# Expert rows scattered in item order and read back by plain transfers, in a two-layer decoder step

## What is computed

```
logits = h @ w_router + b_router;  probs = softmax(logits)
group  = the one of 4 expert groups whose two best probs sum highest
gates  = the two best experts of that group, weighted to sum 1
y = sum over the two experts e:  gates[e] * ((silu(h @ w_gate[e]) * (h @ w_up[e])) @ w_down[e])
```

## Time and profile before

| | us |
|---|---|
| median of 3 runs | 2256.04 |
| lowest, highest | 2251.12, 2267.28 |
| profiled execution, its own time | 2252.14 |
| its span (first to last instruction) | 2250.4 |

### The profile page before, as it was taken

How to read it: one execution, slowest core, us unless ns; L and a number is a source line. 1 busy time by engine, 2 the same in 40 slices (tenths; PEclk the granted TensorE clock), 3 DMA queues, 4 the chain that set the end, 5 groups by cost and what they waited for, 6 DMA issues and landing times.

```text
span 2250.4 us, 22594 instructions
## 1 busy us (share of the span) xinstructions
PE 1770.5 (79%) x7649; PEld 1214.5 (54%) x7649; DVE 1216.2 (54%) x1760; ACT 860.5 (38%) x1035; POOL 221.7 (10%) x242
## 2 busy tenths in 40 slices
PE   3799898889898994299999179995577942999990
PEld 0556335565335774187877057663344742787870
DVE  1332344332335337398988572237733373989886
ACT  1222222222223202088887212223343022887861
POOL 0000000000010000322221200000000003122201
PEclk7799999899999995599999589976776956999995
DMA  8344184344173423399998512122001243999973
GB/s 306 142 170 171 56 289 161 128 164 171 56 280 113 142 95 113 103 347 393 393 393 330 197 57 75 60 81 75 1 1 38 68 178 130 368 393 392 393 292 123
DMA packets 199192, 418.66 MB, mean 186 GB/s; under 512 B 16909, under 2 KB 21069, under 8 KB 199094
## 3 DMA queue, kind: packets, MB, share of 16 engines
q1 hardware_dynamic: 169730, 322.26, 40.2%
q0 software_dynamic: 22128, 73.53, 8.8%
q10 hardware_dynamic: 7254, 21.84, 2.9%
HBM read 367.56 MB, written 50.03 MB: 186 GB/s over the span
## 4 chain that ended last, share of the span: by engine, by line
PE 59%; DVE 14%; DMA 10%; issue 5%; ACT 4%; DVEq 4%; POOL 1%; ACTq 1%; POOLq 0%; SPq 0%
PE bank L652 24%; PE bank L998 18%; PE bank L636 3%; DMA RING<-in_w_in_ret 3%; PE bank L936 3%; DMA RING<-in_w_gate 2%; PE bank L674 2%; ACT WH L1478 2%; PE bank L921 1%; PE bank L910 1%; DVEq L2415 1%; DVE RINGR L1866 1%; POOL slot_d L1764 1%; DVE X L1925 1%; DVE X L1923 1%
## 5 line engine op out<-in xcount | busy, mean ns | idle before, releaser
L2260 DVE TENSOR_TENSOR WL<-RING,WH 128x2048 fp32r<-128x2048 f32 x192 | 435.8, 2289 | 71.4 <-ACT WH L1478 69.6
L652 PE MATMUL bank<-RINGR,HTH 128*128 128x512 f32 (+2 forms) x1440 | 468.9, 410 | 2.9 <-ACT M L1403 2.3
L1478 ACT ACTIVATE WH<-RING 128x2048 fp32r<-128x2048 f32 x192 | 364.5, 1915 | 113.4 <-PE bank L998 92.8
L636 PE MATMUL bank<-cst,M 128*128 128x128 f32 (+3 forms) x721 | 124.1, 307 | 263.9 <-DMA M<-h_d,slot_c 81.2
L652 PEld LDWEIGHTS bank<-RINGR,HTH 128*128 128x128 f32 (+1 forms) x1440 | 249.0, 181 | 117.1 <-issue 34.2
L652 PE MATMUL bank<-RINGR,HTL 128*128 128x512 f32 (+3 forms) x720 | 288.7, 402 | 0.0
L636 PEld LDWEIGHTS bank<-cst,M 128*128 128x128 f32 (+3 forms) x721 | 99.0, 164 | 298.0 <-DMA M<-h_d,slot_c 81.4
L1866 DVE TENSOR_TENSOR RINGR<-RING,RINGR 128x2048 fp32r<-128x2048 f32 (+1 forms) x48 | 105.8, 2211 | 225.5 <-ACT RINGR L1279 198.9
L998 PE MATMUL bank<-WH,HGH 128*128 128x512 f32 x512 | 204.4, 399 | 3.0 <-DVE HGL L2271 3.0
L998 PE MATMUL bank<-WH,HGL 128*128 128x512 f32 x512 | 201.3, 393 | 0.0
L998 PE MATMUL bank<-WL,HGH 128*128 128x512 f32 x512 | 200.9, 392 | 0.0
(11 more groups left out here) (285 smaller groups left out, 2417.2 us busy)
## 6 DMA issues: line engine op xcount, KB each, us to landing
RING<-in_w_gate SPq DMA_DIRECT2D x64, 1024.0 KB, 11.0
RING<-in_w_up SPq DMA_DIRECT2D x64, 1024.0 KB, 12.2
RING<-in_w_down SPq DMA_DIRECT2D x64, 1024.0 KB, 11.0
RING<-in_w_mod SPq DMA_DIRECT2D x48, 1024.0 KB, 7.5
RING<-in_w_in_ret SPq DMA_DIRECT2D x24, 1024.0 KB, 9.3
RING<-in_state_ret SPq DMA_DIRECT2D x16, 1024.0 KB, 7.1
out_ret_sample<-RING POOLq DMA_DIRECT2D x16, 1024.0 KB, 6.6
RING<-in_w_in_dsa SPq DMA_DIRECT2D x10, 1024.0 KB, 5.1
```

Source lines behind the costliest of these rows:

```text
L636: last = pe.transpose(d_, s_, ident[0:r, 0:r])
L652: last = pe.matmul(out, x_[:, c, :], w_[:, c, :], start=start and c == n == 0, stop=stop and c == 3 and n == 2)
L1478: act.activation(WH[:, u % SPLIT, :, :], raw(u % RAW), ACT.Copy).then_inc(S("hi_rdy"), 1)
L2260: TT(WL[:, u % SPLIT, :, :], raw(u % RAW), WH[:, u % SPLIT, :, :].bitcast(F32), ALU.subtract)\
```

## The change

The buffer `h_d` becomes as large as `y_d`, 128 x 24 rows of 4 KB, and is filled with zeros at the start, behind the fill of `y_d` and on the same semaphore; the two waits for `y_zero` ask for both. POOL no longer stores the tiles of h, and no token numbers are kept. When the destinations are known (`dest_rdy`, a new semaphore ahead of the rest of `route`), ten indirect transfers scatter the rows of `HN` itself to both destinations. For each item a plain transfer on POOL's queue then reads its 128 rows, 96 KB apart; a small copy of zeros and the drain in front of it stay. `HN` has five buffers, over `WL`'s units 2 and 3 and the first row buffer, so VectorE makes the low parts of units 2 and 3 only after the first `take_rows` and after `scattered`. In layer 1's `modulate` a wait for the stores of k and v is added, since `HN` lies over them; the input `tok` isn't loaded.

```diff
-N_CONST = 5
+N_CONST = 4
...
-        h_d = dram("h_d", (TOK, D))
-        slot_d = dram("slot_d", (P * ITEMS, 1), I32)
+        h_d = dram("h_d", (P * ITEMS, D))
+        h_items = h_d.rearrange("(p i) d -> p i d", i=ITEMS)
...
-        HN = [view(2 * SPLIT * UW, D), view(2 * SPLIT * UW + D, D)]
+        HN = [view((2 * SPLIT - 2) * UW + t * D, D) for t in range(TILES)]
...
                     if mod_at == EARLY:
-                        act.wait_ge(S("y_zero"), 16)
+                        act.wait_ge(S("y_zero"), 32)
                     take_part(mod_at, MP[mod_at % 2], bank[7])
...
-            act.dma_start(tok[:, :], A["tok"]).then_inc(S("const_in"), 16)
...
-            pool.dma_start(slot_d.rearrange("(p i) o -> p (i o)", p=P), zero_i[:, :]).then_inc(S("slot_zero"), 16)
+            pool.dma_start(h_items, zero_f.rearrange("p (o d) -> p o d", o=1).to_broadcast([P, ITEMS, D])).then_inc(S("y_zero"), 16)
...
             def experts(l):
                 m = 2 * l + 1
-                for t in range(TILES):
-                    pool.wait_ge(S("hn"), TILES * m + t + 1)
-                    pool.dma_start(h_d[cols(t), :], HN[t % 2][0:rows(t), :]).then_inc(S(f"h_st{t % 2}"), 16)
-                pool.wait_ge(S("slot_zero"), 16)
-                pool.wait_ge(S("tables"), l + 1)
+                pool.wait_ge(S("y_zero"), 32)
+                pool.wait_ge(S("dest_rdy"), l + 1)
                 for k in range(2):
                     for t in range(TILES):
                         R = rows(t)
-                        pool.indirect_dma_start(out=slot_d, out_offset=bass.IndirectOffsetOnAxis(ap=dest_i[0:R, k, t:t + 1], axis=0),
-                                                in_=tok[0:R, t:t + 1], in_offset=None).then_inc(S("scattered"), 16)
+                        pool.indirect_dma_start(out=h_d, out_offset=bass.IndirectOffsetOnAxis(ap=dest_i[0:R, k, t:t + 1], axis=0),
+                                                in_=HN[t][0:R, :], in_offset=None).then_inc(S("scattered"), 16)
+                pool.wait_ge(S("tables"), l + 1)
                 pool.wait_ge(S("scattered"), 16 * 2 * TILES * (l + 1))
-                pool.dma_start(slot_i[:, :], slot_d.rearrange("(p i) o -> p (i o)", i=ITEMS)).then_inc(S("slots_in"), 16)
-                for par in range(2):
-                    pool.wait_ge(S(f"h_st{par}"), 16 * (l + 1) * tiles_of[par])
-                pool.wait_ge(S("slots_in"), 16 * (l + 1))
                 first, last = pairs(pool, l)
                 def gather(j, k):
                     pool.wait_ge(S(f"hg_ps{j}"), (first + k) * 2 + 2)
-                    nc.gpsimd.tensor_tensor(slot_c[:, j:j + 1], slot_i[:, bass.ds(k * 2 + j, 1)], zero_i[:, 0:1], ALU.add)
+                    nc.gpsimd.tensor_tensor(turn_c[:, j:j + 1], zero_i[:, 0:1], zero_i[:, 0:1], ALU.add)
                     pool.drain()
-                    pool.indirect_dma_start(out=HG[j], out_offset=None, in_=h_d,
-                                            in_offset=bass.IndirectOffsetOnAxis(ap=slot_c[:, j:j + 1], axis=0))\
-                        .then_inc(S(f"rows_in{j}"), 16)
+                    item = k * 2 + j
+                    src = h_items[:, item:item + 1, :] if isinstance(item, int) else h_items[:, bass.ds(item, 1), :]
+                    pool.dma_start(HG[j], src.rearrange("p o d -> p (o d)")).then_inc(S(f"rows_in{j}"), 16)
...
             def modulate(m, t):
                 if t == 0:
                     dve.wait_ge(S("bc_in"), 64 * m + 64)
+                    if m == 3:
+                        dve.wait_ge(S("kv_st"), 16 * 3 * TILES)
...
-                if t >= 2:
-                    dve.wait_ge(S("ht_ps"), 2 * TILES * m + 2 * (t - 1))
-                    if m % 2:
-                        dve.wait_ge(S(f"h_st{t % 2}"), 16 * ((m // 2) * tiles_of[t % 2] + t // 2))
...
-                    dve.tensor_copy(dest_i[:, k, :], r1)
+                    last = dve.tensor_copy(dest_i[:, k, :], r1)
                     D_()
+                last.then_inc(S("dest_rdy"), 1)
...
-                first = pairs_before(dve, l)
-                for u in range(SPLIT):
-                    low_unit(first, u)
+                start = pairs_before(dve, l)
                 first, last = pairs(dve, l)
...
-                take_rows(0, first)
+                for u in range(SPLIT):
+                    if u == 2:
+                        take_rows(0, first)
+                        dve.wait_ge(S("scattered"), 16 * 2 * TILES * (l + 1))
+                    low_unit(start, u)
                 with dve.Fori(0, last) as k:
                     pair(first + k, False)
```

More of the change, by code:

```diff
@@ L187, in trunk @@
         rotc = sb("rotc", [P, 2, TILES, P])
-        tok = sb("tok", [P, TILES], I32)
         zero_i = sb("zero_i", [P, ITEMS], I32)
@@ L200, in trunk @@
         np_i = sb("np_i", [P, DEPTH], I32)
-        slot_i = sb("slot_i", [P, ITEMS], I32)
-        slot_c = sb("slot_c", [P, 2], I32)
+        turn_c = sb("turn_c", [P, 2], I32)
         dest_c = sb("dest_c", [P, 2, TILES], I32)
@@ L714, in modulated @@
                         transposes([bank[6 + g][:, q * R:(q + 1) * R] for q in range(4)],
-                                   [HN[t % 2][0:R, (4 * g + q) * P:(4 * g + q + 1) * P] for q in range(4)], "ht_ps")
+                                   [HN[t][0:R, (4 * g + q) * P:(4 * g + q + 1) * P] for q in range(4)], "ht_ps")
                     if m % 2 and t:
@@ L1850, in modulate @@
                     dve.wait_ge(S("bc_in"), 64 * m + 64)
+                    if m == 3:
+                        dve.wait_ge(S("kv_st"), 16 * 3 * TILES)
                 R = rows(t)
                 sc_, sh = (SC[:, 0, :], SC[:, 1, :]) if t == NT else SCALE_SHIFT if m else (BC[:, 0, :], BC[:, 1, :])
-                if t >= 2:
-                    dve.wait_ge(S("ht_ps"), 2 * TILES * m + 2 * (t - 1))
-                    if m % 2:
-                        dve.wait_ge(S(f"h_st{t % 2}"), 16 * ((m // 2) * tiles_of[t % 2] + t // 2))
-                TT(HN[t % 2][0:R, :], X[0:R, t, :], sc_[0:R, :], ALU.mult)
+                TT(HN[t][0:R, :], X[0:R, t, :], sc_[0:R, :], ALU.mult)
                 dve.drain()
-                TT(HN[t % 2][0:R, :], HN[t % 2][0:R, :], sh[0:R, :], ALU.add).then_inc(S("hn"), 1)
+                TT(HN[t][0:R, :], HN[t][0:R, :], sh[0:R, :], ALU.add).then_inc(S("hn"), 1)
             def low(*key):
```

## The result

The changed kernel takes 2276.85 us in the median of seven executions (2269.28 to 2279.77), the kernel before 2256.04 us (2251.12 to 2267.28). The ratio is 1.0088, with a 95% interval of 1.0070 to 1.0106: slower by 0.9%, some 20 us. The forecast was 2273 us. The profiled execution took 2269.28 us, its span is 2267.7 us, 17.3 more than before; the granted clock is 0.865 in the mean, 0.867 before.

A forecast was written before the change was run, and what follows sets the result against it. No engine was taken to bound the kernel throughout; the experts' loop runs at the transfers' pace. Fill +25, gain before the experts -8, loop 0 make +17 us on the 2256.0 us median: 2273 us, range 2256 to 2287.

The forecast's parts named there:

- The fill (+25): Start of layer 0: ScalarE waits for the 12.58 MB fill until 122 us, delaying its split by 25 us.
- Whether loads or fill go first hardly matters: Start of layer 0: the order of fill and ring loads is nearly indifferent, since ScalarE needs both before its split.
- No place where the delay is caught up: After the start of layer 0: nothing later absorbs the fill's delay, so all +25 us stay.
- Rival (a): Later slack absorbs the fill's delay, leaving only the 8 us gain: 2248 us; sign: split under 8 us late; chance 0.10.
- The gain before the experts (8 us): Routing to first expert rows: 4.0 us shorter in layer 0, 4.7 in layer 1, less about 0.3 each; 8 us.
- I take a gain of 0.8 here in layer 0 and 1.5 in layer 1: Before the experts: the last row scatter lands 0.8 us earlier in layer 0 and 1.5 us earlier in layer 1.
- The read-back (2.2 us): Before the experts: reading back the token table and issuing that read go away, saving 2.2 us a layer.
- The standing time: Before the first rows: POOL's standing between small copy and first row transfer stays 7.20 and 4.40 us; other end 0.83.
- (b): Before the experts: the ten row scatters land 5 us later a layer than taken, +27, 2283 us; chance 0.20.
- (c): Before the experts: POOL's standing time belongs to the table's transfers and falls to 0.83 us, +7, 2263 us; chance 0.14.
- (d): Experts' loop: plain reads of rows 96 KB apart take twice as long, adding 43 us, 2316 us; chance 0.03.
- The loop (0): Experts' loop: same bytes at the pace of the transfers, so no change, within 5 us either side.

The follow-up runs named there:

- experiment 1: The kernel before plus only the 12 MB zero fill, into a buffer nothing reads, and the wait for both fills: 2280.75 us against 2253.88, ratio 1.0105.
- experiment 2: The changed kernel with the large fill from its own zero tile and semaphore, ScalarE waiting for the first fill alone, bias rows behind it: 2280.24 us, one execution.
- experiment 3: The changed kernel with the large fill on its own tile and semaphore, and the two bias rows issued ahead of it: 2265.16 us, one execution.
- experiment 7: The changed kernel with VectorE waiting for `scattered` before all four low halves, not only the last two: span 2261.8 us, one execution.
- experiment 6: The changed kernel without the small copy and drain ahead of each layer's first two row transfers: span 2260.3 us, one execution.
- experiment 9: The changed kernel with one more drain on POOL, ahead of its waits for the routing: 2271.21 us, span 2269.6 us, one execution.
- experiment 10: The kernel before with one more drain on POOL, behind the five stores of h: 2247.93 us against 2255.86, ratio 0.9966.

## Why the prediction was right, and where not

**The fill (+25): right.** Measured +23.9 at the split and, in experiment 1, the whole loss. The fill and the loads moved their 13.4 MB at 418 to 420 GB/s and not at the 393 of the loop's mix, and the wait ended at 120.7 and not at 122. The bias rows in POOL's queue, named in the text, are worth 3 to 5 us of it (experiments 2 and 3, one execution each).

**"Whether loads or fill go first hardly matters": right for the change, wrong as a rule.** It holds because ScalarE needs both. It hid that the loads get a third of the bytes beside the fill and not half, since the two move equal numbers of packets, of 2 and of 4 KB, which is why taking the wait away alone gave back little (experiment 2), and why my own expectation of 104 us there failed.

**No place where the delay is caught up: right.** Rival (a) decided at a split less than 8 us late; it was 23.9 late. 22 of it were still there at 300 us, so some 2 us of slack there was, right behind the split. What shrank later, 3.3 us, was the clock's, not slack in the work.

**The gain before the experts (8 us): the right sign, half the size.** Measured 4.3 us. The term that failed is "I take a gain of 0.8 here in layer 0 and 1.5 in layer 1" for the last scatter. It landed 21.4 us after the last `dest_i` and not 20.6: 0.8 later. The issue was right: it starts 0.9 us after the last `dest_i` and not 3.0, two are slow where I took three, and the last comes 14.4 us after the last `dest_i`, as worked out (14.3), but I had let the transfers run at 393 GB/s throughout. They fell to 262 and 101 beside the slow issues (experiment 7), with no rows at all from 934 to 936 us, and the last scatter took 6.97 us to land. Second, the plain transfer of rows took 4.0 us and not the 3.2 that I took from the 2.9 us of the earlier trace rows; the gathers' own 4.12 and 4.26 were the nearer rows. The read-back (2.2 us) went as counted. The standing time fell by 0.5 in each layer, which the prediction kept whole; the six transfers that POOL no longer issues explain it.

**Rivals.** (b), scatters 5 us later a layer than taken, was true in part: the last lands 1.6 us later than taken in layer 0 and 2.6 in layer 1 (22.1 us after the last `dest_i`, where it was 21.0 before and 1.5 less was taken). (c), the standing time belongs to the table, was false: it is the drain's (experiments 6, 9 and 10), and stayed. (d), the wide pitch: no sign of it, the loop's rate is unchanged and a row transfer takes what a gather took.

**The loop (0): right.** From the first `HGL` to the landing of the last store the two kernels differ by 0.3 us in layer 0 and 0.8 in layer 1.

**The total.** Forecast 2273, measured 2276.85. By the profiled executions +17.3 was measured and +17 forecast, but the measured terms are +23.9 and -4.3, which make 19.6. The fill was taken 1.1 us too high and the gain 3.7 too high, and the 2.3 us between 19.6 and 17.3 are the clock's steps and the little slack behind the split. That the two totals meet within 0.3 us is luck; the medians differ by 20.8.

## What to carry to other kernels

A large fill or copy is not free because its data isn't needed for long: put it where the trace shows the transfers idle, since beside weight loads it takes most of the rate and the load is what comes late. If the two must meet, compare the sizes of their packets: in these traces each queue got as many packets as the other, so the one with the larger packets got the bytes. Look for a standing time between an instruction and the next transfer in which neither an engine nor a queue moves: here it was a drain whose time grew with the transfers issued since the last drain, and one more drain in an idle stretch took 8 us off. Where the issue of indirect transfers lies on the path, keep VectorE's two-input work, and the loads that it releases, out of that stretch.

## What was not expected of the hardware

- Three ring loads of 1 MB beside the fill of 12 MB had 134 of 410 GB/s; a load took some 29 us and not 10. Beside three copies from HBM to HBM of 4 MB one took 43.66 us. In both cases the two queues moved nearly equal numbers of packets (1011 and 1013, 273 and 271), of 2 KB for the loads, 4 KB for the fill and up to 32 KB for the copies.
- POOL's drain takes about 0.63 us and 0.082 us for each transfer that POOL has issued since its last drain, also for those that have long landed: 7.20 us for 80, 1.45 for 10, 1.56 for 11. Four kernels had less, as though a 12 MB fill had cleared up what lay before it (5.05 us with 74, 54 of them behind the fill).
- The drain also waits for a transfer of POOL's in flight: between the first two row transfers of layer 0 stands one drain, and the second is issued at 944.60 and 960.66 us in the two kernels, 0.8 and 0.6 us after the first has landed (943.82 and 960.07). Without the drain (experiment 6) it is issued 0.69 us behind the first.
- The issue of an indirect scatter takes 0.95 us alone and 1.8 to 2.8 us beside VectorE's subtractions, and the rows wait with it: from 934 to 936 us none moved, where 360 GB/s moved without the subtractions.
